# A two-layer hybrid encoder step on one core: a feed-forward step cut 256 + 384, weights split earlier, six gate halves before the attention items

## The reference, cut to what matters

```
h = rmsnorm(x)                       # 640 x 1024
proj = h @ w_in                      # q, k, v, indexer and latent columns
ya, yb, yc = fox(proj), dsa(proj), mla(proj)      # three attention branches
g = sigmoid(h @ w_gate)              # 640 x 3072
x = x + (ga*ya@w_fox_out + gb*yb@w_dsa_out + gc*yc@w_mla_out) @ w_o
h2 = rmsnorm(x)
gt, up = split(h2 @ w_ffn_in)        # 2 x 2816 columns
x = x + (silu(gt) * up) @ w_ffn_out
```

## Time and profile before

| what | us |
|---|---|
| median of three runs | 2342.72 |
| lowest, highest | 2341.63, 2344.75 |
| the profiled execution | 2343.62 |
| its span, first to last instruction | 2341.8 |
| PE busy in the span | 2230.8 (95%) |
| DVE busy | 1375.2 (59%) |
| ACT busy | 1022.9 (44%) |
| POOL busy | 410.3 (18%) |

### The profile page before, as it was taken

How to read it: one execution, slowest core, us unless ns; L and a number is a source line. 1 busy time by engine, 2 the same in 40 slices (tenths; PEclk the granted TensorE clock), 3 DMA queues, 4 the chain that set the end, 5 groups by cost and what they waited for, 6 DMA issues and landing times.

```text
span 2341.8 us, 37811 instructions
## 1 busy us (share of the span) xinstructions
PE 2230.8 (95%) x14028; PEld 1952.7 (83%) x14028; DVE 1375.2 (59%) x2734; ACT 1022.9 (44%) x2197; POOL 410.3 (18%) x298
## 2 busy tenths in 40 slices
PE   7988999999999999999999889999999989999999
PEld 6986767778898998989899767677788879899897
DVE  3455755544565865938545557555356468478393
ACT  3243666666633323423232446656566244233241
POOL 1120020020003413413012100201100044043140
PEclk9999999999999999999999999999999989999999
DMA  6222212305132222222242222132142312222222
GB/s 232 79 89 80 76 58 89 99 30 168 37 130 77 73 82 81 83 81 82 77 133 77 72 93 86 51 103 67 40 165 73 107 65 88 76 84 79 82 82 89
DMA packets 101781, 205.67 MB, mean 88 GB/s; under 512 B 37024, under 2 KB 58400, under 8 KB 101472
## 3 DMA queue, kind: packets, MB, share of 16 engines
q1 hardware_dynamic: 101600, 203.25, 26.1%
HBM read 176.64 MB, written 26.57 MB: 87 GB/s over the span
## 4 chain that ended last, share of the span: by engine, by line
PE 86%; ACT 5%; DVE 4%; issue 2%; DVEq 1%; DMA 1%; POOL 1%; SPq 0%; POOLq 0%; ACTq 0%
PE ps L794 25%; PE ps L834 15%; PE ps L1245 7%; PE ps L1246 7%; PE ps L1244 7%; PE ps L843 6%; PE ps L885 3%; PE ps L976 2%; PE ps L993 2%; PE ps L904 1%; PE ps L944 1%; PE ps L1056 1%; PE ps L930 1%; PE ps L1036 1%; PE ps L949 1%
## 5 line engine op out<-in xcount | busy, mean ns | idle before, releaser
L1304 ACT ACTIVATE w_hi<-raw 128x1024 fp32r<-128x1024 f32 (+4 forms) x172 | 171.3, 997 | 428.3 <-PE ps L794 368.8
L834 PE MATMUL ps<-h_hi,w_hi 128*128 128x320 f32 x768 | 251.9, 328 | 0.8 <-ACT g L1304 0.8
L1788 DVE TENSOR_TENSOR w_lo<-raw,w_hi 128x1024 fp32r<-128x1024 f32 (+4 forms) x124 | 139.1, 1123 | 188.3 <-ACT w_hi L1304 184.3
L834 PE MATMUL ps<-h_lo,w_hi 128*128 128x320 f32 x768 | 240.4, 313 | 0.0
L834 PE MATMUL ps<-h_hi,w_lo 128*128 128x320 f32 x768 | 240.2, 313 | 0.0
L1730 POOL TENSOR_TENSOR rsq<-ssq,mhalf 128x12 f32<-128x12 f32 (+3 forms) x56 | 117.0, 2090 | 550.8 <-DVE ssq L1857 461.4
L1246 PE MATMUL ps<-th_hi,op_lo 128*128 128x320 f32 x640 | 198.1, 310 | 0.0
L1245 PE MATMUL ps<-th_lo,op_hi 128*128 128x320 f32 x640 | 198.0, 309 | 0.0
L1244 PE MATMUL ps<-th_hi,op_hi 128*128 128x320 f32 x640 | 197.7, 309 | 0.0
L794 PE MATMUL ps<-w_hi,act_hi 128*128 128x512 f32 x440 | 173.8, 395 | 0.0
L794 PE MATMUL ps<-w_hi,act_lo 128*128 128x512 f32 x440 | 173.8, 395 | 0.0
(11 more groups left out here) (355 smaller groups left out, 5577.2 us busy)
## 6 DMA issues: line engine op xcount, KB each, us to landing
raw<-in_weights SPq DMA_DIRECT2D x212, 512.0 KB, 3.3
gates<-gst SPq DMA_DIRECT2D x72, 160.0 KB, 1.8
g<-gates SPq DMA_DIRECT2D x12, 960.0 KB, 6.4
raw<-in_weights SPq DMA_DIRECT2D x24, 384.0 KB, 3.1
out_y_prompt<-x_sb SPq DMA_DIRECT2D x12, 512.0 KB, 4.9
kc<-in_cache_fox_k SPq DMA_DIRECT2D x16, 384.0 KB, 3.1
vc<-in_cache_fox_v SPq DMA_DIRECT2D x16, 384.0 KB, 3.5
x_sb<-out_y_prompt SPq DMA_DIRECT2D x8, 512.0 KB, 4.2
```

The costliest lines, as they stand in the source:

```text
L834: mm = pe.matmul(ps[:, 5, 0:HALF], w[:, kk * P:(kk + 1) * P], h_pair[x][:, kk, half * HALF:(half + 1) * HALF], start=kk == 0 and n == 0, s ...
L1304: return act.activation(dst, src, ACT.Copy, scale=scale)
L1788: dve.tensor_tensor(low[:, 0:width], raw[raw_slot(c)][:, 0:width], high[:, 0:width].bitcast(F32), ALU.subtract).then_inc(lo_made.sem, 1)
```

## The change

Three things are changed, and the table of buffer places (`HOME`) is laid out anew for them.

1. The first feed-forward step is cut in parts of 256 and 384 tokens (`FIRST_PARTS`). The first part needs only tiles 0 and 1, so it waits for `ln_lo` at 4. The transposes of tile 3 stand in the middle of u = 0, those of tile 4 in the middle of u = 1. ACT and DVE take the two parts out of PSUM by two instructions each.
2. The high and low parts of `C_FF + 2` and `C_FF + 3` are made earlier: on ACT both before `split_t(0)`; on DVE one ahead of the wait for the row sums, the other behind `t_sum(0)`.
3. Six gate halves stand before the items: half 0 after the second tile of transposes, half 1 behind the sum for the weights, halves 2 to 5 after `s` = 2, 4, 6 and 8. 42 are left for the items. Chunk `C_GATE + 2` is loaded ahead of the stores of the sparse branch, and its split and that of `C_GATE + 1` move in the queues of ACT and DVE.

```diff
-GATE_FIRST = 4
+GATE_FIRST = 6
...
+        FIRST_PARTS = (slice(0, 2 * P), slice(2 * P, NTOK))
...
-                for c in (C_GATE, C_GATE + 1):
+                for c in (C_GATE, C_GATE + 1, C_GATE + 2):
                     chunk(c, c % 2)
...
                     gate_store(k)
                     if k == 1:
-                        chunk(C_GATE + 2, 0)
                         chunk(C_GATE + 3, 1)
+                    if k == 4:
+                        chunk(C_GATE + 4, 0)
...
-                        for k in range(GATE_FIRST // 2):
+                        for k in range(1, GATE_FIRST // 2):
                             chunk(C_GATE + 4 + k, k % 2)
...
+                    if t == 0:
+                        pe.wait_ge(proj_out.sem, proj_out.at(L, TT * len(GROUPS)))
+                        gate_half(0)
...
+                gate_half(1)
+
...
-                    if s % 2 and 3 <= s < 3 + 2 * GATE_FIRST:
-                        if s == 3:
-                            pe.wait_ge(proj_out.sem, proj_out.at(L, TT * len(GROUPS)))
-                        gate_half(s // 2 - 1)
+                    if s >= 2 and s % 2 == 0:
+                        gate_half(s // 2 + 1)
...
-                pe.wait_ge(ln_lo.sem, ln_lo.at(L, 2 * TT + 6))
-                for half in range(2):
+                pe.wait_ge(ln_lo.sem, ln_lo.at(L, 2 * TT + 4))
+                for part, cols in enumerate(FIRST_PARTS):
                     for u in range(2):
-                        if half == 0:
+                        if part == 0:
                             pe.wait_ge(lo_made.sem, lo_made.at(L, MADE[C_FF + u]))
                         for kk in range(KD):
-                            if half == 0 and (u, kk) in ((1, 0), (1, 4)):
-                                norm_transposes(1, 3 + kk // 4)
+                            if part == 0 and kk == 4:
+                                norm_transposes(1, 3 + u)
...
+                gate_move(0)
+
...
-                    if s >= 4 and s % 2 == 0 and s // 2 - 2 < GATE_FIRST:
-                        gate_move(s // 2 - 2)
+                    if s % 2:
+                        gate_move(s // 2 + 1)
...
+                hi(C_FF + 2, 0)
+                hi(C_FF + 3, 1)
                 split_t(0)
-                hi(C_FF + 2, 0)
                 plain_silu(0, C_FF)
                 split_t(1)
                 split_t(2)
                 split_t(3)
-                hi(C_FF + 3, 1)
...
+                    if b == 0:
+                        lo(C_GATE + 1, 1)
+                    if b == 4:
+                        lo(C_GATE + 2, 0)
                     if b == 2:
-                        lo(C_GATE + 1, 1)
...
+                ff_lo(C_FF + 2)
                 dve.wait_ge(h_summed.sem, h_summed.at(L, 2 * TT))
                 t_sum(0, h_full[0][:, :, first], h_full[0][:, :, second], h_full[0][:, :, first])
+                ff_lo(C_FF + 3)
                 t_sum(1, h_full[0][:, :, second], h_full[1][:, :, second], h_full[0][:, :, second])
-                ff_lo(C_FF + 2)
...
                 plain_act(0, C_FF)
                 t_lo(1)
-                ff_lo(C_FF + 3)
...
+                dve.drain()
                 plain_act(1, C_FF + 2)
```

More of the change, by code:

```diff
@@ L208 @@
 HOME = {
[L209 to L223, removed]
+    "mix": 0, "th": 0, "cumt": 0, "rope_past": 0, "qz": 0, "sdec": 0, "bkrep_past": 0, "relb": 0, "olt": 2048,
@@ new lines @@
+    "ktbd": 2048, "masks_f32": 2048, "grow": 2304, "p_m": 3328, "biasd": 5120, "ctb": 6656, "dk_past": 6656,
+    "k_mlas": 8704, "dv_past": 10752, "zi": 11648, "ka": 11648, "iktb": 12672, "bvec": 12672, "expd": 14720,
+    "zd": 14848, "logf": 15232, "qzr": 15360, "at_dsa": 15360, "qf": 16256, "kn_mla": 16256, "qn_mla": 17792,
+    "qrope": 19328, "ropet": 22400, "onehot": 22912, "gst": 23936, "bkrep": 26496, "at_fox": 26496, "ikrep": 29056,
+    "ikrep_past": 31616, "sq_a": 34176, "sq_b": 36480, "v_dsa": 38016, "kpe": 39296, "kt": 39936, "xt13": 39936,
@@ L224 @@
+    "at_mla": 109056, "x_squares": 114176, "ub": 114176, "gate_past": 114688, "ik_past": 116224, "g5": 116736,
+    "vc": 116736, "ckvc": 116736, "sums": 118272, "qn_fox": 122880, "probs_t": 124928, "x_sb": 126464, "pen": 133120,
+    "av": 137728, "ckv_new": 138752, "g0": 139264, "p_v": 139264, "ktbm": 139264, "kn_fox": 147072,
 }
@@ L1554, in _ @@
                         act.activation(relu[:, b % 2, 0:PAST + P], ps[:, b % 2, 0:PAST + P], ACT.Relu).then_inc(ix_relu.sem, 1)
-                for k in range(DECB // 2 - 1, GATE_FIRST):
-                    gate_move(k)
                 for step in range(N_ITEMS + 6):
@@ L1634, in plain_silu @@
                     act.wait_ge(act_ready.sem, act_ready.at(L, jg - 1))
-                    act.activation(halves(sg[:, jg % 2, :]), two((3 + 2 * jg) % 4), ACT.Silu).then_inc(silu_ready.sem, 1)
+                    if jg:
+                        last = act.activation(halves(sg[:, jg, :]), two(1), ACT.Silu)
+                    else:
+                        for part, cols in enumerate(FIRST_PARTS):
+                            last = act.activation(sg[:, 0, cols], ps[:, 6 + part, 0:cols.stop - cols.start], ACT.Silu)
+                    last.then_inc(silu_ready.sem, 1)
+                hi(C_FF + 2, 0)
+                hi(C_FF + 3, 1)
                 split_t(0)
-                hi(C_FF + 2, 0)
                 plain_silu(0, C_FF)
@@ L2208, in plain_act @@
                     dve.wait_ge(w_used.sem, w_used.at(L, MADE[c + 1]))
-                    mul(halves(ff_act[:, :]), halves(sg[:, j, :]), two(2 * j))
+                    if j:
+                        mul(halves(ff_act[:, :]), halves(sg[:, j, :]), two(2))
+                    else:
+                        for part, cols in enumerate(FIRST_PARTS):
+                            mul(ff_act[:, cols], sg[:, 0, cols], ps[:, part, 0:cols.stop - cols.start])
                     split_act(j)
                 first, second = slice(0, HALF), slice(HALF, NTOK)
+                ff_lo(C_FF + 2)
                 dve.wait_ge(h_summed.sem, h_summed.at(L, 2 * TT))
                 t_sum(0, h_full[0][:, :, first], h_full[0][:, :, second], h_full[0][:, :, first])
+                ff_lo(C_FF + 3)
                 t_sum(1, h_full[0][:, :, second], h_full[1][:, :, second], h_full[0][:, :, second])
-                ff_lo(C_FF + 2)
                 t_sum(2, h_full[1][:, :, second], h_full[1][:, :, second], h_full[0][:, :, first])
```

12 lines of the change are left out of this document (8 added, 4 removed).

## The result

The changed kernel takes 2326.98 us (median of four runs, 2326.42 to 2328.47), the kernel before 2342.18 in the same round (four runs, 2338.55 to 2344.75): ratio 0.9941, 95% interval 0.9928 to 0.9955. It is 15.2 us faster, where 27.2 were forecast. The time lies inside the range that was given (2301 to 2330), outside the likeliest case's own (2307 to 2323), and nearest to the 2329 of rival 2.

A forecast was written before the change was run, and what follows sets the result against it. PE, busy 95% of the span, was taken to bound the kernel, leaving idle and low-clock time to win. 5.4 + 3.2 + 5.0 = 13.6 us a layer, 27.2 for two, took 2343.6 to 2316.4, forecast as 2315; range 2301 to 2330.

The forecast's parts named there:

- the likeliest case: Whole kernel: the forecast of 2315 us itself, with its own range of 2307 to 2323 and chance 0.58.
- rival 2: Stage before the items, and items: gate halves gain nothing; only A and the lost DMA wait remain, 5.4 + 1.5, 2329; chance 0.17.
- A: Start of the feed-forward: first product 8.1 us earlier, less 2.7 for low clock, 5.4 us a layer; bounds 3.5 to 8.7.
- move inside: DVE's chain from first difference to operand_lo: one weight split leaves, the other only moves within it; 20.7 - 1.8 + 0.1 us.
- B: Between projection and items: first item at 206.4, 3.2 us sooner with two halves more done; bounds 0.5 to 5.5.
- The step that priced the lost wait at its own 3.75: Between projection and items: PE's wait of 3.75 us at 196.88, hung on the load of C_GATE + 2, goes.
- the halves' cover: Between projection and items: two more halves, 7.0 us, fill 1.1 of waiting, so 5.9 later; another 1.5 is taken back.
- C: The items: 42 halves in place of 44, 5.0 us a layer less; bounds 0 and 8.
- 7.0 - 3 + 1: The items: 7.0 us less work, 3 back as odd-step waits, 1 won from a freer DVE: 5.0 us a layer.
- The price of odd steps: Fox items from step 13: halves in odd steps don't cover the wait for ACT's copy; six steps at 0.5, 3 us.
- The 1 us for a DVE without the late split: First items: they find DVE free of the late weight split, worth about 1 us.
- rival 3: Items: halves in odd steps leave pauses ahead of line 976 that lower the clock, 3.5 us each; slower, 2353; chance 0.03.

The follow-up runs named there:

- split behind the sums: Changed kernel, but DVE makes the low part of C_FF + 2 behind the first difference, not ahead of the wait for POOL's row sums: 2328.27 us.
- The load alone: Kernel before, with the load of C_GATE + 2 ahead of the stores, four halves ahead, and the changed kernel's buffer places and added DVE drain: 2326.95 us.
- the even steps with four halves ahead: Kernel with early load, feed-forward edits, four halves ahead and DVE summing tiles 3 and 4, with gate halves 4 to 9 in even item steps: 2300.30 us.
- The last kernel: Not identified in the text: the last one listed has DVE summing three tiles, 2311.01 us; the fastest has gate halves 4 to 9 in even steps, 2300.30 us.
- the parts alone: Kernel with the feed-forward edits alone, minus the early weight splits, so only the parts of 256 and 384 tokens; gates as before: 2335.64 us.
- row sums shared: Kernel with early load, feed-forward edits and four halves ahead, with DVE adding up tiles 3 and 4 and POOL only tiles 0 to 2: 2312.33 us.

## Why the prediction was right, and where its size was off

**A, forecast 5.4 a layer, measured 3.7 and 4.4.** The mechanism was right in each step: line 1227 starts at once, no wait for w_lo, a new wait for `op_lo` with a clock of 0.50 behind it. Counted from the end of tile 2's transposes, the product was to come at 35.8 us (772.4 - 736.6) and came at 37.2. Two terms made the 1.4. The row sums ended 0.3 later: POOL was held up by 1.0 (with the split behind the sums this goes) and won back 0.7, where I had taken up to 1.2 and 0.6 and let the two cancel. And DVE's chain from the first difference to `op_lo` took 20.1 us (750.00 to 770.06) in place of 19.0: I let the second split only "move inside" at its old price, but it and the two differences behind it now ran beside POOL's sums of weights (2.15, and 5.09 for two). The wait was therefore 5.7 and not 4.7, and the low clock cost 2.9 and 2.6 against 2.7. Matmuls of 256 and 384 columns start every 0.117 and 0.173 us, so their time went with the columns, the lower of the two bounds given.

**B, forecast 3.2, measured 3.4 and 2.0.** The first item was to start at 206.4 and started at 206.25. But this was a sum of two things that I did not price apart. The load alone is worth 7.5 and 6.3, because the low clock behind the relu wait goes with it (3.2 us at 0.50 and 4 at 0.65, some 3 us lost); two halves ahead, with the splits that move with them, cost 4.1 of the 7.0 us that they last. The stage of before took 53.7 to 56.3 us in the four kernels that have it, so these are good to about 1. The step that priced the lost wait at its own 3.75 left out the low clock behind it, and the halves' cover was taken too high. The two errors cancelled, and that the first item came at the forecast time is luck.

**C, forecast 5.0, measured 0.3 and 3.3.** (The items are 88, not the 80 written ahead of the prediction: 32 fox, 32 latent and 24 sparse ones. No sum used the number.) This is the step that failed: "7.0 - 3 + 1". By the means over the kernels it is worth 0.9. In both layers 5.3 of the 7.0 us came back as idle time (26.6 to 31.9 and 27.2 to 32.5). The price of odd steps was near, but low: nine more waits at line 977, 4.7 us a layer (11.4 against 6.7), where I took six for 3. The 1 us for a DVE without the late split was not seen; the wait at the items' start stayed 2.11. In layer 1 another 1.2 came back as busy time, as 7.0 us of work went and PE was busy for 5.8 less: its window 450 to 470 ran at 0.91 where before had 1.00. When the steps are put back, the waits behind ACT's copy fall by 6 us, but a wait of 3.0 and the low clock come at the start, and the time falls by one a layer at most. I read this so: in these items a half is not only 3.5 us of work. It fills a step whose length ACT and DVE set, and taking it out shortens the step only where PE is the last. The even steps with four halves ahead bear this out; with six it is not shown. Rival 2 said this for B and C together, and was nearest; rival 3's mechanism is in the traces too, in small.

**The sum.** 1.7 and 1.0 less in A, 0.2 more and 1.2 less in B, 4.7 and 1.7 less in C make 10.1. The profiled execution was to take 2316.4 and took 2326.42, 10.0 more. Two thirds of the miss is C.

**What stays open.** Why the clock fell behind 2.58 us and not behind 2.52, and why the clock falls more often in the items of one execution than of another, when the waits are the same. The last kernel still has waits that no run tried to move, 3.6 us for `av` among them.

## What to carry to other kernels

Before moving work to fill a wait, take away what makes the wait: here one load issued ahead of a store was worth as much as the whole change, and the filler then cost more than it saved. Filler work is worth its length only in the steps where its engine would wait, so choose the steps by the waits that the trace shows, one by one, and not by an even spread. When a wait ends in another queue, follow that queue to its slowest member (POOL's ten row sums) and share its work, before rearranging what stands around it.

## What the runs showed of the hardware

- The clock of PE fell behind waits much shorter than the 4.96 us of the earlier trace rows, and not behind all. It was at 0.50 or 0.51 behind 5.69 us (770, changed kernel), 5.05 us (754.6, the parts alone) and 2.58 us (754, split behind the sums); it stayed at 1.00 behind 2.52 us (766, the parts alone) and 2.11 us (764.55, row sums shared). The length of the wait alone does not decide: behind the 2.10 us at 219.72 in the kernel before it was 0.61 over 219 to 223. There PE had been busy for 2.62 of the 4 us from 215, with short score matmuls and transposes; ahead of 764.55 it ran the dense matmuls of the second step without a gap. Where the clock fell behind the product it cost 2.6 to 2.9 us. Cutting the wait from 5.7 to 2.1 us was worth 4.3 us a layer, more than its 3.6.
- DVE instructions with two operands in SBUF and POOL's sums hold each other up, and the one that starts second pays. POOL's first sum of weights took 2.19 us where it started at 750.47, in the middle of DVE's difference (750.00 to 751.49), and 1.27 where it started at 751.45, 0.1 ahead of DVE's two splits, which then took 4.47 in place of 2 x 1.23. Over the row sums the loss was 1.01 on POOL and 0.22 on DVE, together the 1.23 of the split. Row sums on DVE took 1.10 us each beside POOL's and 0.62 with POOL idle. The Trainium skill, "SBUF — State Buffer", section "SBUF: two separate sides", says that such a pair excludes one another for the whole of the instruction that comes first; the trace agrees in these numbers.
